# The dilated attention mixer as one stage, with pieces, rotation and softmax rearranged

## Chip, core and metric

One core of a Trainium2 chip runs the whole program. The time is device microseconds from start to end of one execution; less is better. TensorE is written PE, VectorE DVE, ScalarE ACT, GpSimd POOL, SyncE SP.

## What is computed

The program takes 256 tokens of width 1024 through two transformer layers of one kind (feed-forward, three-branch token mixer, feed-forward) and two of another: a state space mixer, an expert layer, a **dilated attention mixer**, an expert layer, each with a layer norm behind it. The change is in the dilated mixer alone, which is this:

```python
ATT_HEAD_DIM = 64; ATT_HEADS_PER_GROUP = 8
ATT_PATTERNS = ((128, 1), (512, 4), (2048, 16))      # window, dilation

def _dilated_attention_mixer(x, cos, sin, w_qkv, w_o):
    bsz, s, _ = x.shape
    qkv = (x @ w_qkv).reshape(bsz, s, ATT_N_GROUPS, 3, ATT_HEADS_PER_GROUP, ATT_HEAD_DIM)
    for g, (window, dilation) in enumerate(ATT_PATTERNS):
        q = _apply_partial_rope(qkv[:, :, g, 0], cos, sin)      # first 16 of 64 features are rotated
        k = _apply_partial_rope(qkv[:, :, g, 1], cos, sin)
        o, m, l = _dilated_window_attention(q, k, qkv[:, :, g, 2], window, dilation)
        ...
    wgt = l * jnp.exp(m - jnp.max(m, 0, keepdims=True))
    merged = jnp.sum(wgt[..., None] * o, 0) / jnp.sum(wgt, 0)[..., None]
    return merged.reshape(bsz, s, ATT_OUT_DIM).astype(x.dtype) @ w_o
```

Three patterns have queries, keys and values of their own, 8 heads each. The weights `wgt` are the sums of the exponentials, so the merged result is that of one softmax over the keys of all three patterns.

## The kernel before

**Weights and units.** All weights come through a ring of eight 1 MB slots (`WeightStream`), filled from SP's queue in one fixed order; `s.issue(sp, upto)` issues the loads up to a position and waits, for each, until its slot is released. The 4608 columns of `attn_w_qkv` are 18 pieces of 256, and a piece is two *units*. A unit (`Units`) passes through one of three buffers: ACT rounds it to an upper part (`upper`, L215), DVE subtracts that from the weights to get a lower part (`lower`, L223), and PE multiplies with both (`feature_products`, L278, or `value_products`, L291), 24 matmuls of 256 columns a unit. The buffer of unit n is that of unit n + 3, so ACT's upper part for n + 3 waits for the products of n, and DVE's lower part for ACT.

**Projection block of `dilated_mixer`.** It loops over the pieces in the order of the weights: for each pattern two pieces of queries, two of keys, two of values. PE has four banks of PSUM for them; ACT copies each piece out (L3025). POOL meanwhile finishes the rows of x that the last norm left (`finish_rows`, L999), from the time when the sixth unit of the mixer is split. Behind the loop, DVE computes the angles and reduces them (L3038 to L3049, 18 small instructions, each waiting for the last), and ACT takes sine and cosine.

**Rotation block.** For each of 24 tiles of 128 features by 256 tokens PE multiplies with a fixed matrix (L3063, fp32) and DVE combines it with the tables (L3071, L3073, L3074).

**Attention block** (`attention_stage`). One unit here is one head of one pattern, 24 in all. PE does its scores (L1077), its transposed probabilities (L1088) and its outputs (L1101), DVE adds the mask and takes the largest logit, ACT takes the exponentials. Before and between the units, `keep_clock` has PE multiply zeros.

**Merge block.** DVE weighs and adds the three patterns, PE turns the rows (L1172), and 16 fp32 products of 512 columns with `attn_w_o` (L3153) end the mixer. The norm behind it takes its first half of the tokens as soon as those are complete (DVE L871).

A barrier stands between the blocks: no engine starts the next one before all have ended the last.

**Where its neighbours stand.** The expert stage behind the norm has its own loop over slots; its loads wait for `x_parts`, which the norm signals. `heads_stage`, the mixer of the first two layers, already treats heads in pairs, one on partitions 0 to 63 and one on 64 to 127 (scores L1597, transposes L1629, outputs L1650 and L1652, logits by `tensor_tensor_reduce` L1813, exponentials L1752, scaling L1832), and puts projection products between their steps.

Of the kernel before, what the change touches and what calls it, by code (L numbers as in the profile page):

```python
# [21 lines left out]
P = 128  # L22
# [27 lines left out]
CLOCK_START, CLOCK_UNIT, CLOCK_SHORT = 4096, 384, 512  # L50
# [231 lines left out]

def value_products(c, pe, units, bank):

    for j, n in enumerate(units):
        w = c.units.both(n)
        pe.wait_ge(c.units.split, n + 1)
        for t in range(TT):
            for k in range(4):
                for of_w, of_x in PARTS:  # L290
                    m = pe.matmul(bank[:, t * S:(t + 1) * S], c.xTp[of_x][:, 4 * j + k, t * P:(t + 1) * P], w[of_w][:, k, :],  # L291
                                  start=(j == 0 and t == 0 and k == 0 and (of_w, of_x) == PARTS[0]),
                                  stop=(j == 1 and t == 1 and k == 3 and (of_w, of_x) == PARTS[-1]))
        m.then_inc(c.units.done, 1)
# [108 lines left out]
class Core:  # L403


    def __init__(self, nc, ctx, a, out):
# [69 lines left out]
        self.sc_full, self.s_ready, self.nm_ready = self.heads.scores, self.heads.logits, self.heads.cmp_logits  # L476
        self.p_ready, self.pt_ps, self.pt_ready = self.heads.probs, self.heads.pt_ps, self.heads.probsT
        self.o_ps, self.o_raw = self.heads.out_ps, self.heads.kept
        self.mixT_ps, self.mixT = self.proj.v_ps, self.proj.v_rows
# [525 lines left out]


def keep_clock(c, pe, columns):

    for n in range(0, columns, 512):
        w = min(512, columns - n)
        pe.matmul(c.ps[:, 7, 0:w], c.zeros[:, 0:P], c.zeros[:, 0:w], start=True, stop=True)

class Unit:


    def __init__(self, q, k, nk, bias, values, extra=None, sink=None):  # L1020
        self.q = q
        self.k = k
        self.nk = nk
        self.bias = bias
        self.values = values
        self.extra = extra
        self.sink = sink


def attention_stage(c, units, raw, nm, lsum, before=None):  # L1030

    nc, ps, s = c.nc, c.ps, c.stream
    n = len(units)

    norm = c.norm[:, :, :].rearrange("p k n -> p (k n)")
    sb_s = [norm[:, i * 512:(i + 1) * 512] for i in range(3)]
    sb_pT = [norm[:, 1536:1920], c.take(384)]  # L1040
    mx = [c.take(2) for _ in range(2)]
    c.barrier()

    def seen_keys(u, slot):

        return units[u].nk if slot == 0 else min(units[u].nk, P)

    def lay(u, v, slot):
        nk = units[u].nk
        return v[:, slot * nk:slot * nk + seen_keys(u, slot)]  # L1050


    def blocks(u):
        if units[u].nk == NC_CMP:
            return [(0, 0, 0), (1, 0, P)]
        return [(0, 0, 0), (0, P, P), (1, 0, 2 * P)]

    if True:
        block = c.block

        @block.tensor
        def _(pe):
            keep_clock(c, pe, CLOCK_START)
            for step in range(n + 3):
                u = step
                if u < n:
                    un = units[u]
                    keep_clock(c, pe, CLOCK_SHORT if un.nk == NC_CMP else CLOCK_UNIT)
                    if u >= 2:

                        pe.wait_ge(c.s_ready.sem, c.s_ready.at(u - 1))
                    for slot in range(2):
                        t = 1 - slot
                        o = lay(u, ps[:, u % 2, :], slot)
                        pairs = [(un.q(t), un.k)] + (un.extra(t) if un.extra else [])
                        for i, (lhsT, rhs) in enumerate(pairs):
                            m = pe.matmul(o, lhsT, rhs[:, 0:seen_keys(u, slot)], start=(i == 0), stop=(i == len(pairs) - 1))  # L1077
                    m.then_inc(c.sc_full.sem, c.sc_full.one())
                u = step - 2
                if 0 <= u < n:  # L1080

                    pe.wait_ge(c.p_ready.sem, c.p_ready.at(u + 1))
                    if u >= 2:

                        pe.wait_ge(c.pt_ready.sem, c.pt_ready.at(u - 1))
                    nk = min(units[u].nk, P)
                    for slot, k0, col in blocks(u):
                        m = pe.transpose(ps[0:nk, 2 + u % 2, col:col + P], lay(u, sb_s[u % 3], slot)[:, k0:k0 + nk], c.ident[:, :])  # L1088
                    m.then_inc(c.pt_ps.sem, c.pt_ps.one())
                u = step - 3  # L1090
                if 0 <= u < n:

                    pe.wait_ge(c.pt_ready.sem, c.pt_ready.at(u + 1))
                    if u >= 2:

                        pe.wait_ge(c.o_raw.sem, c.o_raw.at(u - 1))
# [8 lines left out]

        @block.vector
        def _(dve):
            ch = c.dve_chain
            for step in range(n + 4):
                u = step  # L1110
                if u < n:
# [2170 lines left out]
```

## Time and profile before

| | us |
|---|---|
| median of 3 runs | 2946.88 (2946.37 to 2947.45) |
| the profiled execution | 2947.6 |
| its span, first to last instruction | 2945.7 |

| stretch of the span | from | to |
|---|---|---|
| attention projections | 2190 | 2292.4 |
| rotation | 2292.4 | 2324 |
| attention units | 2324 | 2401 |
| merge and output projection, to the norm | 2401 | 2426 |
| second expert stage, without its start and end | 2442 | 2886 |

The profile is read by stretches here. In a window's row stand its start and end, its length, the busy us and the instructions of PE, PEld (weight loads), DVE, ACT and POOL, then the granted PE clock (1.00 is 2.4 GHz, 0.50 is 1.2 GHz), the busy share of the DMA engines and GB/s. In a timeline's row stand start, duration, engine, line, operation, tiles and shapes, the count of merged instructions and, in brackets, the idle time before with what ended it. An fp32 matmul stands as two instructions. PE's matmuls overlap, so that distances between starts say more than durations.

### The profile page before, as it was taken

The numbers are of one execution on the slowest core, as the hardware profiler recorded it, in microseconds if no ns is written. First come the engines' busy times: TensorE is split into PE (matmuls) and PEld (weight loads), VectorE is DVE, ScalarE is ACT, GpSimd is POOL, SyncE is SP. The second block draws the span as 40 slices with busy tenths as digits, with TensorE's granted clock in tenths as the row PEclk, the third lists the DMA queues.
The fourth block names the chain that finished last, engine by engine and source line by source line (L and its number), as shares of the span: only waits on it lengthen the run. The fifth ranks groups of instructions, "written<-read, shape, count | busy, mean of one in ns | idle before, by whom it ended". The sixth has DMA issues, their size and how long they took to land. (4 is left out here: it accounts for less than half of the span.)

```text
span 2945.7 us, 40085 instructions
## 1 busy us (share of the span) xinstructions
PE 2694.1 (91%) x16430; PEld 1958.4 (66%) x16430; DVE 1262.7 (43%) x2375; ACT 1000.2 (34%) x1652; POOL 81.3 (3%) x32
## 2 busy tenths in 40 slices
PE   8989999999998999999899889999889787989896
PEld 8978887798998988699787444333359553433332
DVE  5565653656657464465676321111134644111112
ACT  4444552444444464244466211111134232111111
POOL 0001000100101000010100000000010000000000
PEclk9999999999999999999899999999999998999999
DMA  9636533464555742455442489999994018999996
GB/s 308 204 109 184 179 107 129 161 211 149 190 193 140 226 108 98 150 182 188 144 129 101 148 350 421 421 421 421 421 327 137 1 43 350 421 421 421 422 421 283
DMA packets 313985, 695.31 MB, mean 236 GB/s; under 512 B 57104, under 2 KB 242320, under 8 KB 264656
## 3 DMA queue, kind: packets, MB, share of 16 engines
q1 hardware_dynamic: 310896, 682.24, 63.1%
q10 hardware_dynamic: 2912, 10.52, 1.1%
q8 instruction: 134, 2.20, 0.3%
q14 instruction: 43, 0.35, 0.0%
HBM read 691.63 MB, written 1.08 MB: 235 GB/s over the span
## 5 line engine op out<-in xcount | busy, mean ns | idle before, releaser
L278 PE MATMUL ps<-xT_upper,weight_parts 128*128 128x256 f32 (+1 forms) x4656 | 857.5, 287 | 26.8 <-DVE xT_lower L903 12.9
L223 DVE TENSOR_TENSOR weight_parts<-ring,weight_parts 128x1024 fp32r<-128x1024 f32 x447 | 578.7, 1299 | 474.8 <-ACT weight_parts L215 474.4
L278 PEld LDWEIGHTS ps<-xT_upper,weight_parts 128*128 128x128 f32 (+1 forms) x4656 | 729.9, 192 | 45.7 <-issue 21.7
L278 PE MATMUL ps<-xT_lower,weight_parts 128*128 128x256 f32 (+1 forms) x2328 | 662.6, 285 | 0.0
L215 ACT ACTIVATE weight_parts<-ring 128x1024 fp32r<-128x1024 f32 x447 | 470.9, 1055 | 552.2 <-PE ps L278 319.9
L278 PEld LDWEIGHTS ps<-xT_lower,weight_parts 128*128 128x128 f32 (+1 forms) x2328 | 445.8, 191 | 0.5
L2612 PE MATMUL ps<-ring,bias_tiles 128*64 128x512 f32 x1024 | 240.9, 596 | 34.9 <-DMA ring<-in_moe_w_gate 19.0
L2612 PE MATMUL ps<-ring,arena 128*64 128x512 f32 x1024 | 239.9, 596 | 34.6 <-DMA ring<-in_moe_w_gate 18.8
L2901 DVE TENSOR_TENSOR bias_tiles<-ps,bias_tiles 128x512 f32<-128x512 f32 x32 | 22.1, 692 | 506.4 <-ACT bias_tiles L2758 506.4
L2662 PE MATMUL ps<-moe_slots,bias_tiles 128*64 128x512 f32 x1024 | 229.0, 595 | 4.4 <-ACT bias_tiles L2761 4.4
L761 PE MATMUL ps<-weight_parts,hidden_upper 128*128 128x512 f32 x704 | 218.3, 391 | 1.7 <-DVE hidden_lower L813 1.7
L2612 PEld LDWEIGHTS ps<-ring,bias_tiles 128*64 128x64 f32 x1024 | 78.7, 137 | 193.7 <-issue 122.5
L2612 PEld LDWEIGHTS ps<-ring,arena 128*64 128x64 f32 x1024 | 75.6, 137 | 195.1 <-issue 127.6
L2758 ACT ACTIVATE bias_tiles<-ps 128x512 f32<-128x512 f32 x32 | 19.1, 598 | 517.5 <-PE ps L2612 517.5
L2662 PEld LDWEIGHTS ps<-moe_slots,bias_tiles 128*64 128x64 f32 x1024 | 75.8, 137 | 133.8 <-issue 120.2
L2914 DVE SCALAR_TENSOR_TENSOR moe_rounded<-ps,arena,moe_rounded 128x512 fp32r<-128x512 f32 x64 | 48.1, 751 | 255.9 <-ACT moe_rounded L2773 255.9
L1670 PE MATMUL ps<-xT_upper,weight_parts 128*128 128x256 f32 x768 | 148.0, 292 | 0.0
L761 PEld LDWEIGHTS ps<-weight_parts,hidden_upper 128*128 128x128 f32 x704 | 128.7, 188 | 28.9 <-issue 3.9
L999 POOL TENSOR_TENSOR x_rows<-x_rows,norm_params 128x1024 f32<-128x1024 f32 x28 | 81.1, 2915 | 2132.5 <-DVE weight_parts L223 2131.9
L761 PE MATMUL ps<-weight_parts,hidden_lower 128*128 128x512 f32 x352 | 137.8, 391 | 0.0
L1670 PEld LDWEIGHTS ps<-xT_upper,weight_parts 128*128 128x128 f32 x768 | 119.8, 192 | 4.0 <-ACT arena L1765 0.3
L1670 PE MATMUL ps<-xT_lower,weight_parts 128*128 128x256 f32 x384 | 109.3, 285 | 0.0
(339 smaller groups left out, 2855.3 us busy)
## 6 DMA issues: line engine op xcount, KB each, us to landing
ring<-in_ffn_w SPq DMA_DIRECT2D x132, 1024.0 KB, 5.1
ring<-in_moe_w_up SPq DMA_DIRECT2D x128, 1024.0 KB, 24.3
ring<-in_moe_w_gate SPq DMA_DIRECT2D x128, 1024.0 KB, 24.4
moe_slots<-in_moe_w_down SPq DMA_DIRECT2D x128, 1024.0 KB, 20.2
ring<-in_w_gate SPq DMA_DIRECT2D x24, 1024.0 KB, 7.5
ring<-in_w_in SPq DMA_DIRECT2D x20, 1024.0 KB, 6.6
ring<-in_ssd_w_in SPq DMA_DIRECT2D x20, 1024.0 KB, 5.3
ring<-in_attn_w_qkv SPq DMA_DIRECT2D x18, 1024.0 KB, 10.9
```

The costliest lines, as they stand in the source:

```text
L215: act.activation(self.part(n, 0), cut(self.stream.slot(pos)), ACT.Copy).then_inc(self.upper_done, 1)
L223: dve.tensor_tensor(self.part(n, 1), cut(self.stream.slot(pos)), self.part(n, 0).bitcast(F32), ALU.subtract).then_inc(self.split, 1)
L278: m = pe.matmul(out[0:rows, :], w[of_w][:, k, :], c.xTp[of_x][:, k, :], start=(k == 0 and (of_w, of_x) == PARTS[0]), stop=(k == KT - 1 and ...
L761: mm = pe.matmul(ps[:, 2 * t + cols, :], h_parts[of_h][:, half, t * P:(t + 1) * P], w[of_w][:, cols * 512:(cols + 1) * 512], start=(n == 0 ...
L999: ins = pool.tensor_tensor(c.x[:, t, :], c.x[:, t, :], c.norm[:, which, :], op)
L1670: mm = pe.matmul(ps[:, 7 - m % 2, 0:S], w[of_w][:, k, :], c.xTp[of_x][:, k, :], start=(k == 0 and (of_w, of_x) == PARTS[0]), stop=(k == KT ...
L2612: mm = pe.matmul(ps[e * SLOTS:(e + 1) * SLOTS, 7 - w, :], xe[m % 2][:, 4 * half + k, e0 + e * SLOTS:e0 + (e + 1) * SLOTS], rows4(piece(q)) ...
L2662: mm = pe.matmul(ps[e * SLOTS:(e + 1) * SLOTS, 7 - half, :], hT[:, kk, e * SLOTS:(e + 1) * SLOTS], rows2(piece(q))[:, kk % 2, half * 512:( ...
L2758: act.activation(sgp, ps[:, 6, :], ACT.Silu).then_inc(K.sg_full, 1)
L2901: dve.tensor_tensor(h, ps[:, 7, :], sgp, ALU.mult).then_inc(K.h_full, 1)
L2914: dve.scalar_tensor_tensor(y_parts[1][:, cols], ps[:, 7 - half, :], gate[:, 0:1], y_parts[0][:, cols].bitcast(F32), ALU.mult, ALU.subtract ...
```

## The change

All four blocks become one, and these things change in it.

- The pieces come in another order: for each half m of the heads, query and key pieces of the three patterns in turn, then the three value pieces.
- The loads of the constants, the angles and sine and cosine stand at the first piece. Each query or key piece is copied to `raw`, and PE's rotation product (now 512 columns, in one bank) stands behind the first unit of the next piece; DVE's three operations (`turn`) stand behind the lower part at the second unit of that piece.
- Heads are treated in pairs on both halves of the array. A step n = 3i + g is pair i in pattern g, with scores (S), logits (L), transposes (T) and outputs (O); there are 12. The maximum runs on over the three patterns, the exponentials (E) and the scaling (P) are one for the pair, and the outputs of the three patterns add up in one bank, already with features on partitions; K keeps them. The merge, the turning of rows and `keep_clock` go.
- These steps are put between the units by hand (`SLOTS_OF`, a table of piece and unit for each engine). The first two pairs are done within the loop, of the last two the steps up to T7; the rest stands behind it, between the products of the output projection.
- PE has two banks for pieces in place of four. `s.issue` covers the loads up to the end of the plan at once, and ACT loads the norm's parameters before its last four copies.

```diff
+        self.order = []
+        for m in range(2):
+            self.order += [(kind, g, m) for g in range(3) for kind in "qk"]
+            self.order += [("v", g, m) for g in range(3)]
...
-            s.issue(sp, plan.proj_end + AHEAD)
+            s.issue(sp, plan.end + AHEAD)
...
+            def rotate(r):
+                pe.wait_ge(K.pieces.sem, K.pieces.at(turn_of[r] + 1))
+                if r == 0:
+                    pe.wait_ge(c.small.sem, c.small.at(48))
                 else:
+                    pe.wait_ge(K.turned.sem, K.turned.at(r))
+                pe.matmul(ps[:, ROT_BANK, :], rotm, raw[r % 2], start=True, stop=True).then_inc(K.rot_ps.sem, K.rot_ps.one())
+            def scores(n):
+                i, g = n // 3, n % 3
+                pe.wait_ge(K.turned.sem, K.turned.at(6 * (i // 2) + 2 * g + 2))
+                if n:
+                    pe.wait_ge(K.logits.sem, K.logits.at(4 * SCORES_ORDER.index(n)))
+                for slot in range(2):
+                    t = slice((1 - slot) * P, (2 - slot) * P)
...
+                    for h in range(2):
+                        lo = HD * h
+                        m = pe.matmul(ps[:, h, at:at + keys], qk[lo:lo + HD, 8 * g + i, t], qk[lo:lo + HD, 8 * g + 4 + i, 0:keys],
+                                      start=True, stop=True)
+                m.then_inc(K.scores.sem, K.scores.one())
...
+            SLOTS_OF = {(3, 0): "S0", (3, 1): "S3", (5, 0): "S1", (5, 1): "S4", (7, 0): "S2", (7, 1): "S5", (9, 0): "T0", (9, 1): "O0 T1",
+                        (10, 0): "O1 T2", (10, 1): "O2 T3", (11, 0): "O3 T4", (11, 1): "O4 T5", (12, 0): "O5", (12, 1): "S6",
+                        (13, 0): "S9", (14, 0): "S7", (14, 1): "S10", (15, 1): "S8", (16, 0): "S11", (17, 0): "T6", (17, 1): "O6 T7"}
+            turned = 0
+            for p, units in enumerate(plan.units):
+                if p >= 2:
+                    pe.wait_ge(K.pieces.sem, K.pieces.at(p - 1))
+                for j, n in enumerate(units):
+                    if plan.order[p][0] == "v":
+                        value_unit(c, pe, units, j, bank(p))
+                    else:
+                        feature_products(c, pe, n, bank(p)[:, j * S:(j + 1) * S], fresh=(p == 0 and j == 0))
+                    if j == 0 and p >= 1 and plan.order[p - 1][0] != "v":
+                        rotate(turned)
+                        turned += 1
+                    steps(*((w[0], int(w[1:])) for w in SLOTS_OF.get((p, j), "").split()))
+            pe.wait_ge(K.logits.sem, K.logits.at(48))
+            steps(("T", 8), ("O", 7))
+            pe.wait_ge(K.kept.sem, K.kept.at(2))
+            out_rows(0, 0)
+            steps(("T", 9), ("O", 8))
+            out_rows(0, 1)
+            steps(("T", 10), ("O", 9), ("T", 11), ("O", 10))
+            out_rows(0, 2)
+            steps(("O", 11))
+            out_rows(1, 0)
+            out_rows(1, 1).then_inc(s.used, 1)
+            pe.wait_ge(K.kept.sem, K.kept.at(4))
+            out_rows(0, 3).then_inc(c.acc.sem, c.acc.one())
...
+                    if (p, j) == (0, 1):
+                        act.wait_ge(K.trig.sem, K.trig.at(2))
+                        act.activation(sinT, sinT, ACT.Sin)
+                        act.activation(cosT, cosT, ACT.Sin).then_inc(K.trig_act.sem, K.trig_act.one())
...
+            def turn(r):
...
+                dve.wait_ge(K.pieces.sem, K.pieces.at(turn_of[r] + 1))
+                dve.tensor_tensor(out, halves(raw[r % 2]), twice(cosT), ALU.mult)
+                dve.wait_ge(K.rot_ps.sem, K.rot_ps.at(r + 1))
+                ch.link(dve, dve.tensor_tensor(halves(tmp), halves(ps[:, ROT_BANK, :]), twice(sinT), ALU.mult))
+                dve.tensor_tensor(out, out, halves(tmp), ALU.add).then_inc(K.turned.sem, K.turned.one())
...
+            turned = 0
+            for p, units in enumerate(plan.units):
+                for j, n in enumerate(units):
+                    c.units.lower(dve, n + UNITS)
+                    if (p, j) == (0, 0):
+                        angles()
+                        reduced(sinT, 0.0)
+                    if (p, j) == (0, 1):
+                        reduced(cosT, 0.25)
+                    if j == 1 and p >= 1 and plan.order[p - 1][0] != "v":
+                        turn(turned)
+                        turned += 1
+                    for w in SLOTS_OF.get((p, j), "").split():
+                        {"L": logits, "P": probs, "K": keep}[w[0]](int(w[1:]))
+            keep(2)
+            keep(3)
```

DVE's and ACT's tables (`SLOTS_OF` of each) put the logits of a step at the piece and unit of its scores, the exponentials of pairs 0 to 3 at (7, 1), (8, 0), (16, 0) and (16, 1), their scaling at (8, 0), (8, 1), (16, 1) and (17, 0), and ACT's copies of the turned probabilities at the place of the transposes.

## Rows read from the trace of the kernel before

**Rows 1.** The page, first line.

```profile
span 2945.7 us, 40085 instructions
```

**Rows 2.** Windows: us; busy us PE, PEld, DVE, ACT, POOL; clock; DMA share; GB/s.

```profile
2190.00:2292.40 102.40, 102.39 (x858) 102.18 (x857) 54.74 (x53) 45.21 (x52) 12.35 (x4) 0.99 0.49 154
2292.40:2324.00 31.60, 16.75 (x49) 8.82 (x49) 26.78 (x74) 2.65 (x5) 0.00 (x0) 0.92 0.00 0
2324.00:2401.00 77.00, 74.83 (x376) 50.50 (x376) 38.49 (x144) 33.97 (x121) 0.00 (x0) 0.97 0.00 1
2401.00:2426.00 25.00, 15.39 (x33) 7.47 (x34) 7.92 (x19) 2.72 (x4) 0.00 (x0) 0.73 0.33 126
2442.00:2886.00 444.00, 402.47 (x1873) 170.79 (x1872) 66.25 (x152) 59.53 (x79) 0.00 (x0) 0.98 1.01 420
```

**Rows 3.** Timeline, angles and rotation: start us, us, engine, line, operation, shapes.

```profile
2286.33 0.28 DVE L3038 CAST bias_tiles<-bias_tiles 128x256 f32<-128x256 int32 x1
...
2292.11 0.27 PE L291 MATMUL ps<-weight_parts,xT_lower 128*128 128x256 f32 x1
...
2292.62 0.29 DVE L3049 TENSOR_SCALAR arena<-bias_tiles 128x256 f32<-128x256 f32 x1
2293.04 1.28 ACT L3028 ACT_TABLE_LOAD   x1
...
2301.09 0.42 DVE L3071 TENSOR_TENSOR arena<-ps,arena 128x256 f32<-128x256 f32 x1
...
2302.22 0.42 DVE L3071 TENSOR_TENSOR arena<-ps,arena 128x256 f32<-128x256 f32 x1
```

**Rows 4.** Timeline, from the last attention unit to the norm.

```profile
2399.88 0.88 PE L1101 MATMUL ps<-bias_tiles,arena 128*128 128x64 f32 x6
...
2409.92 1.97 PE L1172 MATMUL ps<-ident,arena 128*128 128x128 f32 x8 [9.17 <-DVE arena L3131]
...
2412.58 16.71 PE L3153 MATMUL ps<-ring,arena 128*128 128x512 f32 x32 [0.69 <-ACT arena L1179]
...
2425.96 1.22 DVE L871 SCALAR_TENSOR_TENSOR x_rows<-x_rows,ps 128x1024 f32<-128x1024 f32 x1 [16.09 <-PE ps L3153]
```

**Rows 5.** Timeline of TensorE, layer 1's mixer: scores of two pairs.

```profile
1064.48 0.92 PE L1597 MATMUL ps<-arena 64*128 64x256 f32 x8
...
1071.25 0.92 PE L1597 MATMUL ps<-arena 64*128 64x256 f32 x8
```

**Rows 6.** Timeline of ScalarE and VectorE at the start of the attention projections.

```profile
2193.46 1.06 ACT L215 ACTIVATE weight_parts<-ring 128x1024 fp32r<-128x1024 f32 x1 [1.68 <-PE ps L278]
...
2194.56 1.22 DVE L223 TENSOR_TENSOR weight_parts<-ring,weight_parts 128x1024 fp32r<-128x1024 f32 x1 [1.33 <-ACT weight_parts L215]
...
2196.30 1.06 ACT L215 ACTIVATE weight_parts<-ring 128x1024 fp32r<-128x1024 f32 x1 [1.78 <-PE ps L278]
```

**Rows 7.** Groups of instructions by form: count, busy us, mean ns, idle before.

```profile
L903 DVE TENSOR_TENSOR xT_lower<-arena,xT_upper 128x512 fp32r<-128x512 f32 x36 | 24.0, 687 | 12.4 <-ACT xT_upper L955 12.4
...
L1813 DVE CUSTOM_DVE_ANT_0 norm_params<-ps,bias_tiles 128x256 f32<-128x256 f32 x48 | 20.2, 421 | 20.8 <-PE ps L1607 15.1 <-PE ps L1597 5.6
...
L1752 ACT ACTIVATE norm_params<-norm_params,arena 128x256 f32<-128x256 f32 x64 | 32.1, 502 | 72.6 <-DVE arena L1813 72.6
...
L1832 DVE TENSOR_SCALAR norm_params<-norm_params,arena 128x256 f32<-128x256 f32 x64 | 22.4, 351 | 1.1
```

**Rows 8.** Timeline of VectorE and GpSimd while GpSimd finishes rows.

```profile
244.86 2.11 DVE L1482 TENSOR_TENSOR arena<-arena 128x8 f32<-128x8 f32 x1
...
2201.59 2.41 POOL L999 TENSOR_TENSOR x_rows<-x_rows,norm_params 128x1024 f32<-128x1024 f32 x1 [736.81 <-DVE weight_parts L223]
```

**Rows 9.** Windows of 1 us around a fall and a return of the clock.

```profile
2404.00:2405.00 1.00, 0.00 (x0) 0.00 (x0) 1.00 (x2) 0.00 (x0) 0.00 (x0) 0.71 0.91 365
...
2418.00:2419.00 1.00, 1.00 (x4) 0.52 (x3) 0.00 (x0) 0.00 (x0) 0.00 (x0) 0.96 0.00 0
```

**Rows 10.** DMA issues, attention projections to norm: KB each, us to landing.

```profile
bias_tiles<-in_positions SPq DMA_DIRECT2D x1, 128.0 KB, 4.4
```

More of the change, by code:

```diff
@@ L49 @@
 CONSTANTS = 7 + 2 * DEPTH
-CLOCK_START, CLOCK_UNIT, CLOCK_SHORT = 4096, 384, 512
 NORMS = 10
@@ L475, in __init__ @@
         self.ssd = SsdCounts(self.heads, self.proj)
[L476 to L479, printed above, removed]
+        self.dilated = DilatedCounts(self.heads, self.proj)
         self.router = RouterCounts(self)
@@ L2984, in dilated_mixer, with bank, halves, twice @@
     MAGIC = 12582912.0
-    def bank(g):
-        return ps[:, PROJ_BANKS[g % 4], :]
+    ROT_BANK, OUT_BANK = 5, 4
+    turn_of = [p for p, (kind, _, _) in enumerate(plan.order) if kind != "v"]
+    def bank(p):
+        return ps[:, 6 + p % 2, :]
+    def halves(tile):
+        return tile.rearrange("p (j n) -> p j n", j=2)
+    def twice(table):
+        return bass.AP(table.tensor, table.offset, [table.ap[0], [0, 2], [1, S]])
+    def tiles(p):
+        kind, g, m = plan.order[p]
+        i = 8 * g + 4 * (kind == "k") + 2 * m
+        return qk[:, i:i + 2, :]
+    def logits_of(i, h, slot, g=None):
+        at, n = ((0, S), (3 * S, P))[slot]
+        v_ = logit[i % 2][h][:, at:at + 3 * n]
+        return v_ if g is None else v_[:, g * n:(g + 1) * n]
+    def logits_at(n, j):
+        return K.logits.at(4 * SCORES_ORDER.index(n) + j + 1)
+    def turned_banks(n):
+        return (6, 7) if n >= 8 and n % 2 == 0 else (2, 3)
+    c.small.issued += 48
+    s.release[plan.out[1]] = (c.acc.sem, c.acc.at(2))
     if True:
@@ new lines, in out_rows, with steps @@
+            def out_rows(t, k):
+                if k % 2 == 0:
+                    s.ready(pe, plan.out[k // 2])
+                wo = rows2(s.slot(plan.out[k // 2]))
+                for half in range(2):
+                    m = pe.matmul(ps[:, 2 * t + half, :], qk[:, k, t * P:(t + 1) * P], wo[:, k % 2, half * 512:(half + 1) * 512], start=(k == 0), stop=(k == 3))
+                return m
+            def steps(*items):
+                for what, n in items:
+                    {"S": scores, "T": transposes, "O": outputs}[what](n)
@@ L3014, in _ @@
+            out_rows(1, 2)
+            out_rows(1, 3).then_inc(c.acc.sem, c.acc.one())
         @block.scalar
         def _(act):
[L3016 to L3025 removed]
@@ L3031, in _ @@
+            act.wait_ge(c.rows.sem, c.rows.issued)
+            load_norm(act)
+            for n in range(8, 12):
+                probsT(n)
         @block.vector
```

420 lines of the change are left out of this document (142 added, 278 removed).

## Prediction

> **What bounds the kernel now.** First the span: 2945.7 us, one core [rows 1]; the profiled execution took 2947.6 us, 1.9 us more, and the median of the three timed runs is 0.7 us below it. Then the busy shares by stretch [rows 2]. The 102.4 us of the attention projections have TensorE busy throughout (858 matmul instructions, clock 0.99) and the DMA engines at half load. The next three stretches are the rotation (31.6 us, DMA at 1 GB/s or less), the 24 attention units (77 us) and the merge with the output projection (25 us). The expert stage behind them runs at 420 GB/s, DMA share 1.01: it is bound by its loads. Those start when the normalized x is there, with the same few pieces already in the ring in both kernels, so whatever the dilated mixer saves or loses shifts the expert stage as a block and reaches the end one to one. What is to be priced is the path from the last projection product (2292.11 + 0.27 = 2292.4, [rows 3]) to the first sum of the norm (2425.96, [rows 4]): 133.6 us, in which only the output projection and small pieces keep TensorE usefully busy. The step for the second half of the tokens follows two output steps later in both kernels.
>
> **What is removed.** All 133.6 us of that path: three stage changes, the 64 zero-products that hold the clock, 24 single-head units, 24 rotations serial at 1.13 us (2301.09 to 2302.22, [rows 3]), the three-way merge and two rounds of transposes.
>
> **What is added to TensorE.** (1) A head pair's step. In layer 1's mixer, which already works in pairs on 64-partition halves with projection products between, one pair has one step each of scores, transposes and outputs, and 36 projection matmuls. Its pitch is 1071.25 - 1064.48 = 6.77 us [rows 5]. A unit of 24 such matmuls takes 2196.30 - 2193.46 = 2.84 us [rows 6], so 36 take 4.26, and 2.51 remain: 0.84 us a step, switches and gaps in it. Inside the projection loop stand 12 S, 8 T and 7 O, 27 x 0.84 = 22.7 us. (2) 12 rotations of 512 fp32 columns. The output projection's 16 products of that size took 16.71 us, the first 5.5 us at half clock [rows 4, 9]: (16.71 - 2.7) / 16 = 0.87; with a gap 0.95, so 11.4 us. In the loop: 34.1. (3) Behind the loop, up to the first release: 4 T and 5 O, 7.6 us, and six output steps of two products, 6 x 1.75 = 10.5: 18.1. So if TensorE never waited, the gain were 133.6 - 34.1 - 18.1 = **81.4 us**.
>
> **Where TensorE waits.** In the old loop a unit's end t is followed by ScalarE's upper part (1.06) and VectorE's lower part (1.22, starting 1.10 after it), done at t + 2.4 [rows 6]; nothing else stood on VectorE. The change queues the rotation's arithmetic *behind* the second lower part of a piece: cosine product, sine product, sum, at 0.69 each for 512 columns [rows 7], 2.05 with pipelining, done at t + 4.4. The next rotation on TensorE needs that (one PSUM bank) and stands after one unit, t + 2.84. So TensorE stands 1.5 us, less what score steps fill in, with all later units queued behind it. Walking the slots piece by piece, with S and L (0.42 + 0.28 twice, 1.2 to 1.4 us) where they stand:
> - pieces 4 to 6: 0.7, 1.5, 0.7; S2, which needs the sixth rotation: 1.5; T0: 0.1 (exps of one pair, 768 and 384 columns twice, about 3.1 us from 0.50 for 256 [rows 7]; scaling 2.2 from 0.35 for 256, both in parallel to two value pieces);
> - pieces 13 to 15: 1.1, 1.5, 0.6. Together 7.7 us.
> - S8 stands right behind unit (15,1) and needs the rotation that VectorE does only after that unit: 4.4 us. T6, which needs the exps and scaling of pair 2, comes out level.
> - Start-up. The 18 chained angle instructions (6.6 us, 2286.33 to 2292.9, [rows 3]) were behind the loop; now ten stand ahead of VectorE's lower part for unit 4 and eight ahead of that for unit 5 (units from 0). They wait for the constants, which land 4.4 us after issue [rows 10], near 2195.9, and so end at 2203.6; the two Sin calls end at 2204.4, ScalarE's upper part for unit 5, queued behind them, at 2205.5, the lower part at 2206.7, the next at 2207.9. Then GpSimd's four row operations run, and those lock VectorE out: a 128x8 operation took 2.11 us beside them, waiting for the end of the running one (2.41 when alone) [rows 8]. The first rotation's cosine product so waits to 2210.3 and its sum to 2213.3. TensorE has stood since 2205.8 and goes on at 2214.1, at half clock: rotation 1.8, unit 5 in 4.0, t = 2219.9. Unit 6, then VectorE's second rotation (t + 4.4), rotation, S0 and unit 7 end at 2229.0. Without waits it were 2193.4 + 7 x 2.84 + 3 x 0.95 + 0.84 = 2217.0: 12.0 us, 2.7 of it clock.
> - Clock. TensorE stopped at 2400.8, and the granted clock fell from full to half (2.4 to 1.2 GHz) between 2404 and 2405 (mean 0.71 there); it was back at 2418.0, 5.5 us into dense work [rows 4, 9]. The start-up wait is long enough for that, S8's 4.4 barely; I add 2.2 us there (bounds 0 and 2.7). The 1.5 us waits are not.
> Sum of waits: 12.0 + 7.7 + 4.4 + 2.2 = 26.3.
>
> **Other moves.** Two table loads move: Sin's (1.28, [rows 3]) falls into ScalarE's wait for the angles, Exp's into slack, costing nothing; without that cover 1.3 each. The loads of the next norm's parameters are issued on ScalarE ahead of the copies for T8: 0.8 us, hidden behind two output steps; uncovered, 0.8. On SyncE the two output pieces and the first expert pieces stand in one list behind the ring's releases; nothing waits for them before the tail, and the DMA engines have room. Bounds: nothing, or one piece late in the tail, 5 us. The output of one softmax over three patterns lands already transposed, so no merge is left.
>
> A rule that speaks against the change: GpSimd and VectorE share a port by exclusive lock, held for a whole instruction, when VectorE has two SBUF inputs (Trainium skill, "SBUF — State Buffer", Who interferes with whom). The trace agrees (2.11 us for 8 columns, [rows 8]). Were GpSimd no hindrance, the first rotation would be done at 2210.0, and the start-up term some 4 us less. And the array drains at each change of tile shape (Trainium skill, "TensorEngine Tiling (Array Packing)", Key Properties). The pair's 2.51 us of [rows 5] contain three changes; the new loop scatters its steps and has about ten changes more than that ratio. By the rule, and at no more than 0.2 us each, that would be 2 us more; it isn't in the sum.
>
> **Sum.** Gain 81.4 - 26.3 = 55.1 us; 2947.6 - 55.1 = 2892.5, so **2892 us**.
>
> **Rivals.**
> - *TensorE never waits* (VectorE's arithmetic is faster or overlaps). 2947.6 - 81.4 = 2866. For: VectorE's work in the loop (36 x 1.22 + 12 x 2.05 + 12 x 1.4 + 4 x 2.2 + 6.6 = 101 us) fits into TensorE's 102.4 + 34.1. Against: it is the order that makes the wait, not the amount. 0.10.
> - *Scores wait on the vector queue.* Both score banks serve one step, so each S needs the previous L, and each L stands behind a lower part and a rotation. If each of the 11 later S waits for a full L (1.4), 15.4 us more: 2908. For: L and turn share a queue that already lags. Against: between two S lies a unit of 2.84 us. 0.15.
> - *Slower: the clock stays low.* If the repeated stops held TensorE at 1.2 GHz, the 154.6 us of work (102.4 + 34.1 + 18.1) would take twice as long, with no waits left: 2947.6 - 81.4 + 154.6 = 3021. It decides against the change as soon as more than 55 us of that work run at half clock. For: ten stops of 1.5 us and the fall of [rows 9]. Against: at half clock a unit takes 5.1 us, covers t + 4.4, and the stops vanish, so it heals itself. Layer 1's pairs ran at full clock: 36 matmuls and three steps in 6.77 us [rows 5]. 0.03.
> - *It doesn't do what it says*: heads on both halves run one after the other. A pair's scores would take 1.3, not the 0.92 for eight instructions of [rows 5]; with outputs 15 us more, again near 2908. Or the whole gain is swallowed by a late expert stage, 2947. 0.04 in all, half of it at no change.
>
> **Chances and range.** Forecast 0.68. Faster by over 0.2% (about what a measurement of this kernel can tell from no change): 0.95; within 0.2%: 0.02; slower: 0.03. The range reaches half way to the first rival and over the second, 2872 to 2911.
>
> **What the profile would show.** Right: TensorE idle before the rotation's product, released by VectorE's sum, about 1.5 us, at eight or so of the twelve; one wait of 4 us before the last score step of the first kind (S8); one of over 5 us in the third piece, with the clock at half behind it; loop from 2190 to about 2350, first release some 20 us later; expert stage at 420 GB/s as before, only earlier. Wrong: waits before scores released by the logits, or a low clock beyond the start; a tail much over 20 us; or lower parts that come late, so that plain projection products wait.

## Result and the profile after

| | before | after |
|---|---|---|
| median of the timed runs, us | 2946.62 | 2898.59 (2897.78 to 2899.27) |
| the profiled execution, us | 2947.6 | 2899.1 |
| its span, us | 2945.7 | 2897.2 |

After over before is 0.9837, with a 95% interval of 0.9822 to 0.9852: 48 us faster. The forecast was 2892 in 2872 to 2911, a gain of 55.

The first line of the page, the answer to [rows 1]:

```profile
span 2897.2 us, 39625 instructions
```

The gain is made where it was looked for, in the dilated stage. VectorE's timeline has the first sum of the norm behind it, the answer to the last line of [rows 4], 48.85 us earlier than 2425.96:

```profile
2377.11 1.22 DVE L872 SCALAR_TENSOR_TENSOR x_rows<-x_rows,ps 128x1024 f32<-128x1024 f32 x1 [4.98 <-PE ps L2954]
```

1.12 us of that were there before the stage began (ScalarE's upper part of [rows 6], 2193.46, now starts at 2192.34). Two profiles of the changed kernel itself begin its first rotation at 2197.77 and 2200.14, so a shift of this size comes between two executions of one kernel, and is not counted for the change. The stage gave 47.7 us, and the span ended 48.5 us earlier: what the stage saves does reach the end one to one. The same 444 us of the expert stage, 49 us earlier, are the answer to the last of [rows 2] (columns as there), with the projection loop and its tail ahead of them. Busy times, clock and GB/s are those of before:

```profile
2192.30:2358.50 166.20, 141.24 (x1064) 124.94 (x1063) 97.89 (x205) 64.55 (x101) 11.93 (x4) 0.95 0.33 106
2358.50:2377.10 18.60, 18.30 (x92) 9.78 (x91) 0.85 (x2) 5.64 (x11) 0.00 (x0) 1.00 0.17 57
...
2393.00:2837.00 444.00, 402.54 (x1873) 171.28 (x1872) 66.41 (x152) 59.54 (x79) 0.00 (x0) 0.98 1.01 420
```

In the tail TensorE is busy for 18.30 of 18.60 us. In the loop it lacks 25 us, and the waits view of TensorE (who was waited for: us in total, times, the longest) names them:

```profile
PE ps L2900 <- DVE arena L3072: 16.3, 8, 8.8
PE ps L2914 <- DVE arena L3072: 6.0, 2, 4.4
PE ps L2944 <- DVE arena L3104: 1.7, 1, 1.7
PE ps L2929 <- DVE arena L3098: 0.8, 1, 0.8
PE ps L2944 <- ACT arena L3009: 0.3, 1, 0.3
```

L2900 is the rotation product, L2914 the scores, L2944 the outputs, L2929 the transposes; L3072 is the sum that ends VectorE's rotation arithmetic. TensorE's timeline has each of those waits in its place, 25.1 us in all:

```profile
2197.77 1.02 PE L2900 MATMUL ps<-bias_tiles 128*128 128x512 f32 x2
...
2213.28 2.05 PE L2900 MATMUL ps<-bias_tiles 128*128 128x512 f32 x2 [8.83 <-DVE arena L3072]
...
2224.53 1.10 PE L2900 MATMUL ps<-bias_tiles 128*128 128x512 f32 x2 [1.65 <-DVE arena L3072]
...
2242.43 1.10 PE L2900 MATMUL ps<-bias_tiles 128*128 128x512 f32 x2 [1.66 <-DVE arena L3072]
2243.46 0.92 PE L2914 MATMUL ps<-arena 64*128 64x256 f32 x8
...
2247.34 0.92 PE L2914 MATMUL ps<-arena 64*128 64x256 f32 x8
...
2260.19 0.92 PE L2914 MATMUL ps<-arena 64*128 64x256 f32 x8 [1.60 <-DVE arena L3072]
...
2274.42 0.88 PE L2929 MATMUL ps<-ident,arena 128*128 128x128 f32 x6 [0.82 <-DVE arena L3098]
...
2295.21 0.87 PE L2944 MATMUL ps<-arena,bias_tiles 128*64 128x256 f32 x8 [1.75 <-DVE arena L3104]
...
2340.95 1.65 PE L2914 MATMUL ps<-arena 64*128 64x256 f32 x8 [4.39 <-DVE arena L3072]
...
2346.96 0.92 PE L2914 MATMUL ps<-arena 64*128 64x256 f32 x8
```

Between them lie 0.60 before the rotations at 2234.00 and 2313.63, 0.64 before those at 2251.90 and 2332.66, 1.66 at 2323.19, and 0.30 before O7 at 2359.72. Two score steps with a plain unit between them stand 3.88 us apart (2243.46, 2247.34); behind S8 it is 6.01, since the clock had fallen, as windows of 2 us show (the clock is the third number from the end):

```profile
2336.00:2338.00 2.00, 0.56 (x5) 0.35 (x4) 0.26 (x1) 1.35 (x2) 0.00 (x0) 1.00 0.91 291
2338.00:2340.00 2.00, 0.00 (x0) 0.00 (x0) 2.00 (x3) 0.19 (x1) 0.00 (x0) 0.72 0.55 234
2340.00:2342.00 2.00, 1.05 (x6) 0.88 (x8) 0.86 (x2) 0.00 (x0) 0.00 (x0) 0.50 0.00 0
2342.00:2344.00 2.00, 2.00 (x13) 1.78 (x10) 1.35 (x7) 0.00 (x0) 0.00 (x0) 0.50 0.00 0
```

In what follows "the stage" is the time from the first rotation product to the first sum of the norm, which leaves out what differs ahead of it: 2377.11 - 2197.77 = 179.3 us here, 178.2 in a second profile of the same kernel. The same stretch before is 179.3 + 47.7 = 227.1.

### The profile page after: what moved, and what is told of

Read it like the earlier page. It is cut to its first block, busy times and chain, and to the rows that moved or that the text cites. A ratio compares the mean times of both kernels' runs of the same rounds, so it can differ in the third digit from the quotient of the medians.

```text
span 2897.2 us, 39625 instructions
## 1 busy us (share of the span) xinstructions
PE 2649.9 (91%) x16286; PEld 1929.5 (67%) x16286; DVE 1236.9 (43%) x2298; ACT 987.7 (34%) x1585; POOL 80.9 (3%) x32
## 4 chain that ended last, share of the span: by engine, by line
PE 63%; DMA 20%; DVE 9%; ACT 5%; issue 2%; SPq 0%; ACTq 0%; DVEq 0%
PE ps L277 25%; DMA ring<-in_moe_w_gate 20%; PE ps L762 7%; PE ps L2435 7%; PE ps L1493 4%; PE ps L1533 3%; DVE weight_parts L222 2%; PE ps L2452 2%; PE ps L2485 2%; PE ps L1992 2%; PE ps L1544 2%; PE ps L289 2%; ACT weight_parts L214 1%; DVE tiny L878 1%; PE ps L1420 1%
## 5 line engine op out<-in xcount | busy, mean ns | idle before, releaser
L277 PE MATMUL ps<-xT_upper,weight_parts 128*128 128x256 f32 (+1 forms) x4656 | 861.9, 287 | 27.0 <-DVE xT_lower L904 13.1
## 6 DMA issues: line engine op xcount, KB each, us to landing
ring<-in_moe_w_up SPq DMA_DIRECT2D x128, 1024.0 KB, 24.3
```

The costliest lines, as they stand in the source:

```text
L277: m = pe.matmul(out[0:rows, :], w[of_w][:, k, :], c.xTp[of_x][:, k, :], start=(k == 0 and (of_w, of_x) == PARTS[0]), stop=(k == KT - 1 and ...
```

## Experiments

All start from the changed kernel but the last of the table, which takes one edit out of the combination. Times are medians, ratios are to the kernel before, with 95% intervals. A step, such as S8, T0 or O3, is named as in the section on the change.

| run | us | ratio | stage, us |
|---|---|---|---|
| changed kernel, again | 2899.7 | 0.9846 (0.9829 to 0.9862) | 178.2 |
| rotation arithmetic first | 2878.6 | 0.9779 (0.9762 to 0.9795) | 160.3 |
| GpSimd's rows later | 2896.1 | 0.9839 (0.9822 to 0.9855) | 173.4 |
| S8 one unit later | 2891.5 | 0.9825 (0.9808 to 0.9841) | 173.3 |
| stops filled | 2898.0 | 0.9844 (0.9820 to 0.9869) | 177.8 |
| scores on one half | 2911.0 | 0.9878 (0.9859 to 0.9898) | 188.6 |
| two rotation banks | 2898.2 | 0.9834 (0.9816 to 0.9852) | 174.9 |
| steps behind the loop | 2909.0 | 0.9872 (0.9853 to 0.9891) | 188.8 |
| first copy earlier | 2895.6 | 0.9830 (0.9810 to 0.9850) | 175.8 |
| combination | 2871.1 | 0.9743 (0.9729 to 0.9756) | 149.8 |
| combination, one bank | 2872.6 | 0.9754 (0.9736 to 0.9772) | 151.5 |

What lies outside the stage takes between 2717.9 and 2721.9 us in these profiles, and single executions of one kernel lie up to 15 us apart (2891.3 to 2906.1 with the stops filled). So small edits are read from the stage, whose length two profiles of the unedited kernel, 179.3 and 178.2, give within 1.2 us. Where a difference is given as a span, it is to these two.

**The order on VectorE.** In the loop over a piece's units, `turn` goes ahead of the lower part:

```
                 for j, n in enumerate(units):
+                    if j == 1 and p >= 1 and plan.order[p - 1][0] != "v":
+                        turn(turned)
+                        turned += 1
                     c.units.lower(dve, n + UNITS)
...
-                    if j == 1 and p >= 1 and plan.order[p - 1][0] != "v":
-                        turn(turned)
-                        turned += 1
```

> The changed kernel with one edit: VectorE does a piece's rotation arithmetic before the lower part of the next piece's second unit, not after it. Theory (the order on VectorE's queue makes the waits): the arithmetic is done 4.4 us after the unit that precedes the rotation product instead of 8.2, so TensorE's waits before the rotation product inside the loop (1.65, 0.60, 1.66, 0.64, then 0.60, 1.66, 0.64 us) and the 1.60 before S2 go, 9.05 us in all; S8's wait shrinks from 4.39 to about 0.5 and the clock doesn't fall there (6.0 us with the 2.1 us that half clock cost); at the start one lower part less stands ahead, 1.2 us. Together 16 us: 2883. Rival (the amount of VectorE's work makes them, so a wait that goes comes back as a late lower part before a plain projection product): the sum of waits stays near 25 us and the time within 5 us of 2899. The 1.75 us before the fourth output step stay in both.

2878.6 us, and the stage is 18 to 19 us shorter. The waits view of TensorE, the stage's lines:

```profile
PE ps L2900 <- DVE arena L3072: 7.8, 2, 5.2
...
PE ps L2944 <- DVE arena L3104: 2.0, 1, 2.0
PE ps L2914 <- DVE arena L3072: 0.7, 1, 0.7
PE ps L2929 <- DVE arena L3098: 0.6, 1, 0.6
```

Eight waits before rotations are two, both at the start, and S8 waits 0.71 us instead of 4.39; no plain unit waits for a lower part instead. The same work in another order: it was the order, as the forecast had it, and the rival (the amount) falls. From the first rotation to S0 it gained 2.2 to 4.1 us, where 2.9 were expected (1.2 and the 1.65 before the third rotation): only one of the first three operations now met GpSimd's, but the two lower parts behind them took 6.70 us together beside GpSimd, and the third rotation waited 2.62 us. The rest came in the loop, where a rotation without a wait also takes 0.95 us instead of 1.03 to 1.11.

**GpSimd's rows at unit 22.** `finish_rows(c, pool, plan.units[0][0] + 6)` becomes `+ 22`.

> The changed kernel with GpSimd's four row operations (12 us) begun at unit 22 of the loop instead of unit 6. Theory (the two engines shut each other out at the start): VectorE's first three rotation operations take 0.69 us each instead of 2.83, 0.68 and 2.11, so TensorE's first wait falls from 8.83 to 5.4 us; the clock still falls, for a stop of over 5 us; nothing else moves much, 3.4 us faster: 2895.5. Rival (the constants and the chained angle work set the start-up wait, the lock adds nothing): 8.8 us stay and the time is 2899. The lock's price may come back where the operations now run, as up to 2 us of waits there.

The first wait fell from 8.83 (8.28 in the second profile) to 4.43 us, 1 us below the 5.4 expected, and the stage by 4.8 to 6.0; the median fell by 2.5 to 3.6. VectorE's timeline of the changed kernel, its first rotation:

```profile
2207.56 2.83 DVE L3069 TENSOR_TENSOR arena<-bias_tiles,arena 128x512 f32<-128x512 f32 x1
2210.31 0.68 DVE L3071 TENSOR_TENSOR arena<-ps,arena 128x512 f32<-128x512 f32 x1
2211.03 2.11 DVE L3072 TENSOR_TENSOR arena<-arena 128x512 f32<-128x512 f32 x1
```

and of this run:

```profile
2207.78 0.68 DVE L3069 TENSOR_TENSOR arena<-bias_tiles,arena 128x512 f32<-128x512 f32 x1
2208.39 0.68 DVE L3071 TENSOR_TENSOR arena<-ps,arena 128x512 f32<-128x512 f32 x1
2209.10 0.69 DVE L3072 TENSOR_TENSOR arena<-arena 128x512 f32<-128x512 f32 x1
```

Alone every one takes its own time; beside GpSimd those with both inputs in SBUF take up to 2.2 us more, and L3071, which reads PSUM and SBUF, takes no more. That is the exclusive lock on the shared port (Trainium skill, "SBUF — State Buffer", Who interferes with whom), and the trace agrees with its condition on two SBUF inputs. The price moved with the rows: a rotation at 2289.47 waited 1.72 us, which had not waited before.

**S8 one unit later.** On TensorE `(15, 1): "S8", (16, 0): "S11"` becomes `(16, 0): "S8", (16, 1): "S11"`, and the logits on VectorE likewise.

> The changed kernel with the score step S8 and its logits one unit later (and S11 with its logits one unit later). Theory (S8's wait is VectorE's rotation arithmetic, and the fall of the clock there is the price of that stop): the unit that stood behind S8 runs in the wait; 1.9 us of the 4.39 remain, the clock stays at full, and the 2.1 us lost on S8 and on the unit behind it are gone: 4.6 us faster, 2894.5. The exponentials of pair 2 start later, but T6 comes out level. Rival (pair 2's chain of logits, exponentials and scaling is what the end of the loop hangs on): T6 waits as much as S8 did, about 4 us, and the time stays at 2899.

S8 waited 1.61 us, the clock stayed at 1.00 from 2330 to 2344, T6 waited 0.47. The stage is 4.8 us shorter than in the second profile, whose first wait (8.28 us) is nearest to this one's (8.12), and 6.0 shorter than in the first. So S8's place cost what was said, about half of it clock: its wait is 2.8 us shorter, and S8 to S11 takes 3.87 us instead of 6.01.

**The stops filled.** Eight products of 512 columns before the second rotation, four before S8.

```
+            def keep_busy(n):
+                for _ in range(n):
+                    pe.matmul(ps[:, OUT_BANK, :], rotm, raw[0], start=True, stop=True)
...
+                if r == 1:
+                    keep_busy(8)
...
+                if n == 8:
+                    keep_busy(4)
```

> The changed kernel with 8 idle rotation-sized products (512 columns) on TensorE before the second rotation and 4 before S8, into a bank that nothing uses then. They do no work: they only fill the two long stops. Theory (behind both stops TensorE works at half clock for some microseconds, and that is all that is lost there beside the stops themselves): the waits' ends stay where they were, the clock stays at 1.0, and 2.9 us at the start and 2.1 us at S8 come back: 2894. Rival (the slow unit behind a stop is slow for late weights, not for the clock; or the products outlast the stop): no gain, 2899, with the unit behind S8 still at 4.4 us.

Behind S8 the next unit was back at full speed: S8 to S11 took 3.85 us instead of 6.01, so what was slow there was the clock. At the start the unit pair behind the stop was also at full speed, but the expectation fails: windows of 2 us around the *next* two short stops have the clock falling there.

```profile
2222.00:2224.00 2.00, 0.25 (x3) 0.05 (x1) 1.97 (x4) 1.06 (x1) 0.00 (x0) 1.00 0.52 178
2224.00:2226.00 2.00, 1.94 (x4) 0.50 (x6) 1.05 (x1) 0.00 (x0) 0.00 (x0) 0.58 0.00 0
...
2242.00:2244.00 2.00, 0.45 (x1) 0.30 (x2) 1.97 (x4) 1.05 (x1) 0.00 (x0) 1.00 0.02 6
2244.00:2246.00 2.00, 2.00 (x10) 1.04 (x8) 0.54 (x1) 0.00 (x0) 0.00 (x0) 0.70 0.11 22
```

Those stops were 1.81 and 1.66 us long, and some 3 us went there (a rotation, a score step and a unit took 0.7, 0.7 and 0.2 us more at the first; a step and a unit 0.6 and 1.0 more at the second). The stage is 0.4 to 1.6 us shorter instead of 5.

**Both heads on one half of the array.** In `scores`, `lo = 0` for both heads; this kernel leaves out the second head's own scores.

> The changed kernel with the scores of both heads of a pair taken from the same 64 partitions, so both score products use the same half of TensorE's array (the second head's scores are those of the first: this part of the result is left out). Theory (the two halves work at the same time): a score step of eight instructions grows from 0.85 us to about 1.3 + 0.2 = 1.5, 12 steps of which lose 0.6 each, 7.7 us, less 2.5 where a wait for the rotation's arithmetic stood behind them anyway: 2904. Rival (the halves run one after the other as it is): the step stays at 0.85 and the time at 2899.

TensorE's timeline:

```profile
2248.79 1.57 PE L2914 MATMUL ps<-arena 64*128 64x256 f32 x8
```

The step takes 1.50 us to the next unit instead of 0.85: the two halves do work at the same time, and twelve paired score steps save 7.8 us. The time rose by 11 to 12, not by the 5 expected. The waits behind the steps shrank as expected (0.60 and 0.64 us are gone in four places), but behind a stop of 1.66 us the clock stayed at half for 7 us: the unit between the first two score steps took 5.19 us instead of 3.03, and the first of them 2.44. Behind S8 it cost 3.7 us (S8 to S11 took 8.27 us, two other score steps with a unit between them 4.53), where the two profiles without the edit have 2.1 and 2.9.

**Two banks for the rotation.** The output bank is lent to the rotation. Six of the twelve rotations wait for the arithmetic of the one before the last, and the second for none.

```
+                elif r in (1, 2, 3, 4, 5, 10, 11):
+                    if r >= 2:
+                        pe.wait_ge(K.turned.sem, K.turned.at(r - 1))
                 else:
                     pe.wait_ge(K.turned.sem, K.turned.at(r))
```

> The changed kernel with two PSUM banks for the rotation product (the bank of the outputs lends itself while no output step is under way), so a rotation waits for the arithmetic of the one before the last; VectorE's order is as it was. Theory (VectorE's order makes the waits, the single bank only shows them): waits of 0.6 before rotations go, but those of 1.65 move from the rotation to the score step right behind it, which needs the same arithmetic, and S2's and S8's stay: 2 us in the loop. At the start the second rotation doesn't wait, the fifth unit runs in that time, and the stop moves behind the third rotation, S0 being ready near 2220 instead of 2225.6: 5 us. Together 2892. Rival (the one bank is the cause): all waits before rotations and scores go except S8's, 20 us less: 2879.

TensorE's scores, which have nothing to do with that bank, now wait:

```profile
2224.38 1.65 PE L2920 MATMUL ps<-arena 64*128 64x256 f32 x8 [6.71 <-DVE arena L3078]
...
2242.23 0.92 PE L2920 MATMUL ps<-arena 64*128 64x256 f32 x8 [0.71 <-DVE arena L3078]
...
2338.49 1.65 PE L2920 MATMUL ps<-arena 64*128 64x256 f32 x8 [4.40 <-DVE arena L3078]
```

(L3078 is the same sum as L3072.) The stage is 3.3 to 4.5 us shorter. At the start S0 comes 1.9 to 3.8 us sooner, but the unit behind it runs at half clock, and at S3 nothing (against the second profile) to 1.9 us is left. In the loop the waits of 0.60 and 0.64 go in three places, and two of 1.66 pass from the rotation to the score step behind it as 0.71, the rotation itself being done meanwhile: 3.8 us of waits, and 1.6 lost again to the clock behind O3. The rival's 20 us are not there. The single bank took part in the short waits, but S2's and S8's stand with two banks, and the order alone, with one bank, leaves 0.71 of the 11.8 us that TensorE waited for this arithmetic behind S0.

**The steps of pairs 2 and 3 behind the loop.** S6 to S11, T6, O6, T7 and what VectorE and ScalarE do for them follow the last unit; each engine keeps its order.

> The changed kernel with all steps of head pairs 2 and 3 (six score steps, T6, O6, T7 and the vector and scalar work between them) behind the projection loop instead of in it. Theory (the steps' chain of scores, logits, exponentials and scaling is what the loop hides): the loop gets 13 us shorter (8.4 us of steps and 6.5 us of S8's stop and clock go, waits before rotations grow by 1.7), but behind it six scores and six logits alternate for 15 us and exponentials, scaling and two transposes add 6.5, with the clock falling in it, 3 us: 2899 + 11 = 2910. Rival (the change gains by its form alone, pairs and one softmax; placing it in the loop adds only waits): no more than 2899.

2909.0 us. TensorE's timeline behind the loop:

```profile
2346.89 0.92 PE L2914 MATMUL ps<-arena 64*128 64x256 f32 x8 [1.39 <-DVE arena L3091]
...
2354.30 1.65 PE L2914 MATMUL ps<-arena 64*128 64x256 f32 x8 [1.63 <-DVE arena L3091]
...
2362.69 1.54 PE L2929 MATMUL ps<-ident,arena 128*128 128x128 f32 x6 [3.47 <-DVE arena L3101]
```

Scores and logits alternate, then everything waits for exponentials and scaling, at half clock from the fifth score step on (its row is 1.65 long). Placing half of the steps in the loop is worth 10 us, though S8's stop is gone here; some 38 us of the change's gain stay without it, and no run splits those further.

**The first copy earlier.** On VectorE `(11, 0): "K0"` becomes `(10, 1): "K0"`.

> The changed kernel with VectorE's copy of pair 0's output (K0) one unit earlier, right behind the output step that it waits for. Theory (the fourth output step waits for that copy, and the copy stands one unit too late in VectorE's queue, behind a lower part): the wait of 1.75 us before the fourth output step goes or shrinks to about 0.3 (the rotation arithmetic stays in its place), and the stage is 1.5 us shorter. Rival (another thing ends last there, as the arithmetic of the rotation before it): the wait stays and its releaser is another row.

The wait before the fourth output step is gone, and the stage is 2.3 to 3.5 us shorter, 1.75 of it this wait. So that wait, which the forecast did not have, was the copy's place in the queue.

**The combination.** Rotation arithmetic first, rows at unit 22, two banks, the copy earlier, and on ScalarE:

```
-                    if (p, j) == (0, 1):
+                    if (p, j) == (1, 0):
                         act.wait_ge(K.trig.sem, K.trig.at(2))
                         act.activation(sinT, sinT, ACT.Sin)
```

> The changed kernel with five edits: VectorE's rotation arithmetic ahead of the lower part (as in the first run), GpSimd's rows at unit 22, two banks for the rotation, ScalarE's two Sin calls behind the upper part of the next unit, and the first copy of an output (K0) one unit earlier on VectorE. Theory (order and bank at the start, K0 for the output step): of the 25.1 us of waits and 5.0 us of half clock of the changed kernel, S8's 0.7, T0's 0.6, the last output's 0.3 and at most 3 us at the start stay; 25 us less than 2899: 2874, and 4 to 5 less than the run with the first edit alone (2878.6), since the start-up stop of 5.2 us and its 2.5 of clock lose most and the 2.0 before the fourth output step all. Rival (the start is bound by the angle chain and the constants whatever is moved): the stop of 5 us stays in another place and the time is within 2 us of 2878.

2871.1 us, 0.9743 of the kernel before. The waits view of TensorE, the stage's lines:

```profile
PE ps L2920 <- DVE arena L3078: 0.7, 1, 0.7
PE ps L2935 <- DVE arena L3104: 0.7, 1, 0.7
PE ps L2906 <- ACT bias_tiles L3034: 0.7, 1, 0.7
...
PE ps L2950 <- DVE arena L3110: 0.3, 1, 0.3
PE ps L2950 <- ACT arena L3015: 0.3, 1, 0.3
```

2.7 us of waits are left of 25.1, and the clock stays at 1.00 in all windows of 2 us at the start (2200 to 2216) and around S8 (2310 to 2320). Next, which of its edits the start needs:

> The combined version (2871) with the single bank for the rotation again; VectorE's order, GpSimd's rows, ScalarE's Sin calls and the copy stay as there. Theory (order is what counts, the second bank is needed nowhere once the arithmetic is early): the first rotation's arithmetic is done 1.0 us after TensorE wants the second rotation, against the 0.65 us that it waited anyway, and nothing else moves: 2872, within 1.5 us. Rival (the second bank is what took the stop away at the start): a stop of over 3 us there and 1 to 3 us of half clock behind it: 2876 or more.

2872.6 us; the start-up stop is 2.34 us instead of 0.65 (1.0 was expected), and the clock stays at full. The rival's 3 us and half clock are not there: the second bank is worth 1.7 us of the stage once the order is right. And the yardstick:

> The changed kernel as it is, on the same chip and in the same rounds as the two before it, as their yardstick: 2898.6 by its times so far. What may differ from the first profile of it is the clock: the stops of 1.6 to 1.8 us, behind which it stayed at full there, were followed by half clock in one place each of three other runs (1 to 4 us lost). Theory (it is chance within the same kernel): the sum of waits is 25 us within 1, and the stage's length differs by what is at half clock. Rival (those edits did it): the clock shows the same two falls as before.

Its waits are the same within 0.6 us (8.28 instead of 8.83 at the first, the rest within 0.03). Its clock cost 1.5 us at the start and 2.9 at S8, where the first profile has 2.9 and 2.1. No short stop was followed by half clock here either. So the clock's cost differs by 1 us between executions of one kernel. That the falls behind short stops are chance as well is not shown: they came in three profiles of edited kernels and in neither of the unedited one.

## Why the prediction was right, and where 7 us went

The stage gained 47.7 us; 55.1 were forecast. Term by term, in us:

| term | forecast | measured |
|---|---|---|
| 27 steps in the loop | 22.7 | 24.3 |
| 12 rotations | 11.4 | 13.1 |
| tail to the first release | 18.1 | 18.3 |
| start-up, with its clock | 12.0 | 13.4 |
| waits for the arithmetic, and T0 | 7.7 | 8.2 |
| S8 | 4.4 | 4.4 |
| clock at S8 | 2.2 | 2.1 |
| waits of O3 and O7 | 0 | 2.1 |
| sum | 78.5 | 85.9 |

- **What bounds it** held: the stage's gain arrived whole at the end.
- **A step at 0.84** was taken from layer 1's pairs as a mean. The rows have 0.85 for scores, 0.80 for outputs and 0.63 for transposes; but a unit beside a step takes 3.01 to 3.04 us instead of 2.84 (2243.46 + 0.85 to 2247.34 is 3.03). 12 x 1.04 + 8 x 0.63 + 7 x 0.80 + 7 x 0.17 = 24.3. This is the place where the rule on the array's change of tile shape would show (Trainium skill, "TensorEngine Tiling (Array Packing)", Key Properties), and the 2 us by that rule were left out of the sum. The rows agree in size (1.6 us). That it is the drain is not shown: no run changed the number of shape changes alone.
- **A rotation at 0.95** is right where nothing stops: 0.95 and 0.96 in the combination. Behind a stop it is 1.03 to 1.11. The term's 13.1 is what the other terms leave; the twelve rotations' own rows, with units at 2.84, come to an estimated 12.4, and 0.7 us stay without a place.
- **VectorE's queue, t + 4.4,** was the main mechanism, and the rows follow the walk: 0.60, 1.66, 0.64 where 0.7, 1.5, 0.7 stood, 1.60 at S2 for 1.5, 4.39 at S8 for 4.4; only the fourth of them came out smaller (0.60 for 1.1). The run with the order changed took them away.
- **Start-up:** the stop ended at 2213.28; 2214.1 less the 1.1 of the earlier start is 2213.0. GpSimd's lock added to it as described, 4.4 us by the run with the rows late (3.9 against the second profile), "some 4 us" in the text. Too small was what followed: the stop was 8.8 us, not 8.3, and the rotation and two units behind it ran 2.9 us late through the clock (1.5 in the second profile). The forecast says 2.7 of its 12.0 are clock, but its own steps (a rotation in 1.8 and a unit in 4.0, against 0.95 and 2.84) hold 2.0.
- **"The 1.5 us waits are not" long enough for the clock to fall** is true of both profiles of the changed kernel and false as a rule: in three other profiles it fell behind stops of 1.66 to 1.81 us.
- **The clock at S8,** 2.1 us for 2.2, came so close by luck: the second profile has 2.9, above the bound of 2.7.
- **Missed:** O3's wait for the copy K0. The prediction walked rotations, scores and scaling through VectorE's queue, but not the copies. K0 stood one unit behind its output step, behind a lower part. This is the step of the working that failed, and it cost 1.75 us. The other 5 of the 7 us missing are sizes, nearly all of them too small, so that the forecast held by its mechanism and not by errors that cancel.
- **At nothing:** Sin's table load, the norm's load and the late expert pieces cost nothing that the waits view shows. Exp's load did. "Into slack" was wrong, and with it the 0.1 us at T0, which waited 0.82. ScalarE's and VectorE's timeline of the changed kernel ahead of it:

```profile
2265.77 1.28 ACT L3001 ACT_TABLE_LOAD   x1
...
2270.12 1.05 ACT L214 ACTIVATE weight_parts<-ring 128x1024 fp32r<-128x1024 f32 x1
...
2271.20 1.23 DVE L222 TENSOR_TENSOR weight_parts<-ring,weight_parts 128x1024 fp32r<-128x1024 f32 x1 [3.33 <-ACT weight_parts L214]
...
2272.55 1.81 DVE L3098 TENSOR_SCALAR arena<-arena 128x768 f32<-128x768 f32 x4
```

  The exponentials took the 3.1 us put down (2267.07 to 2270.12), the scaling less than its 2.2. But the load stands ahead of both, the next upper part stands behind the exponentials, and VectorE's lower part, which waits for that, stands ahead of the scaling. Of the load's 1.28 us, 0.7 reached T0. That is read from the queues; no run moved the load.

- **What the profile would show:** TensorE does wait at eight of the twelve rotations, but "about 1.5 us" fits three of them (1.65 and 1.66); four waited 0.60 to 0.64. The tail is the 18.6 us forecast as "some 20"; the loop ends at 2358.5, not "about 2350".
- **The range** reaches, at 2872, over three quarters of the way to the first rival (2866), not half way as it says; half way is 2879. Nothing here hangs on it.

The rivals. *TensorE never waits* (2866): not this kernel, with 25.1 us of waits. The combination has 2.7 us of waits and 2871; its stage gains 227.1 - 149.8 = 77.3 us, where 81.4 less those waits and the 1.8 us mis-sized in steps and tail give 76.9. *Scores wait on the vector queue*: no score step waited for logits (L3088) in the loop; it happens where no unit stands between them (1.38 to 1.63 us a step, in the run with the steps behind the loop). *Clock stays low*: no; in the changed kernel every fall was over within about 10 us. *Halves one after the other*: no, 0.85 against 1.50 us.

## What to carry to other kernels

When work of one engine moves into another's loop, walk each engine's queue in its written order and ask of every entry what stands ahead of it; copies count as much as arithmetic. Here VectorE had time for all of its work, and the order of two entries cost 18 to 19 us. A second buffer helped little against an order: it took 3.3 to 4.5 us, and the longer waits moved to the next reader of the same result.

## What the runs showed of the hardware

- TensorE's clock fell to half behind stops as short as 1.66 us, four times in three profiles; in the changed kernel it stayed at 1.00 behind stops of the same length. The stop of 1.75 us before O3 is the same in the changed kernel and in the run with two banks, and windows of 2 us behind it differ. The changed kernel, whose stop ended at 2295.21 (its windows up to 2302 have 1.00 as well):

```profile
2294.00:2296.00 2.00, 0.79 (x8) 0.57 (x8) 1.06 (x2) 0.00 (x0) 0.00 (x0) 1.00 0.00 0
```

The run with two banks, whose stop ended at 2293.15:

```profile
2292.00:2294.00 2.00, 0.85 (x7) 0.70 (x8) 1.01 (x2) 0.00 (x0) 0.00 (x0) 0.86 0.00 0
2294.00:2296.00 2.00, 2.00 (x13) 1.67 (x10) 0.00 (x0) 0.03 (x1) 0.00 (x0) 0.50 0.00 0
```

- Filling a stop with products did not pay: what it gave back was lost behind the next short stop, and the stage changed by about 1 us.
- A VectorE operation with one input in PSUM ran at its own 0.68 us beside GpSimd's row operations, while its neighbours with both inputs in SBUF took 2.83 and 2.11 us instead of 0.68 and 0.69.
